# Six half-array matmuls in place of four whole-array ones in the rotary part of the attention scores of a hybrid encoder layer

## The reference, cut to what matters

```
q_b = concat([q_b[..., :128], rope(q_b[..., 128:], positions)], -1)
k_b = concat([k_b[..., :128], rope(k_b[..., 128:], positions)], -1)
s = einsum('bhqd,bhkd->bhqk', qblk, k_t) / sqrt(192)
p = softmax(s, -1)
o = einsum('bhqk,bhkd->bhqd', p, v_t)
```

## Time and profile before

| | |
|---|---|
| median of 3 runs | 1947.18 us (1946.17 to 1947.29) |
| the profiled execution: span from first to last instruction | 1945.4 us |
| PE busy | 1877.6 us, 97% |
| PE weight loads | 1593.0 us, 82% |
| DVE busy | 1391.9 us, 72% |
| ACT busy | 1049.2 us, 54% |
| granted TensorE clock, mean | 0.987 |

### The profile page before, as it was taken

How to read it: one execution, slowest core, us unless ns; L and a number is a source line. 1 busy time by engine, 2 the same in 40 slices (tenths; PEclk the granted TensorE clock), 3 DMA queues, 4 the chain that set the end, 5 groups by cost and what they waited for, 6 DMA issues and landing times.

```text
span 1945.4 us, 26995 instructions
## 1 busy us (share of the span) xinstructions
PE 1877.6 (97%) x9388; PEld 1593.0 (82%) x9388; DVE 1391.9 (72%) x1955; ACT 1049.2 (54%) x1726; POOL 135.6 (7%) x147
## 2 busy tenths in 40 slices
PE   7999999999999999999999999994799999999998
PEld 7988888888878888888888888884688888888886
DVE  4578777778855656657766348646799898998986
ACT  6476566555552434344434223321577777877775
POOL 1121101011000000000000000000000101001010
PEclk9999999999999999999999999997899999999999
DMA  6110000000321202022344463534899999999993
GB/s 208 44 43 6 24 23 18 23 23 20 125 61 33 66 22 68 20 76 87 123 165 147 150 197 109 192 130 194 320 377 400 391 401 399 390 400 389 400 391 77
DMA packets 147480, 327.55 MB, mean 168 GB/s; under 512 B 18080, under 2 KB 72736, under 8 KB 147232
## 3 DMA queue, kind: packets, MB, share of 16 engines
q1 hardware_dynamic: 142640, 309.59, 42.9%
q0 software_dynamic: 4752, 16.78, 3.4%
HBM read 287.92 MB, written 38.40 MB: 168 GB/s over the span
## 4 chain that ended last, share of the span: by engine, by line
PE 91%; DVE 5%; ACT 2%; issue 1%; DMA 1%; POOL 1%; SPq 0%; DVEq 0%; ACTq 0%; POOLq 0%
PE ps L1078 24%; PE ps L1080 24%; PE ps L1079 24%; PE ps L1067 7%; PE ps L1163 4%; PE ps L1371 1%; PE ps L1202 1%; PE ps L1201 1%; PE ps L1383 1%; PE ps L1355 1%; PE ps L1525 1%; PE ps L1381 1%; DVE top_i L2476 1%; DVE top_v L2475 1%; DVE affT L2478 1%
## 5 line engine op out<-in xcount | busy, mean ns | idle before, releaser
L1649 DVE TENSOR_TENSOR w_lo<-w_raw,w_hi 128x1024 fp32r<-128x1024 f32 x384 | 442.7, 1220 | 54.8 <-ACT w_hi L3052 54.7
L3052 ACT ACTIVATE w_hi<-w_raw 128x1024 fp32r<-128x1024 f32 x384 | 370.8, 1053 | 12.1 <-DMA w_raw<-in_w_gate_e 11.8
L1078 PE MATMUL ps<-w_hi,xeT_hi 128*128 128x512 f32 x512 | 201.2, 393 | 1.8 <-DVE xeT_lo L1649 1.0
L1080 PE MATMUL ps<-w_hi,xeT_lo 128*128 128x512 f32 x512 | 199.7, 390 | 0.0
L1079 PE MATMUL ps<-w_lo,xeT_hi 128*128 128x512 f32 x512 | 199.2, 389 | 0.0
L1649 DVE TENSOR_TENSOR d_lo<-d_raw,d_hi 128x1024 fp32r<-128x1024 f32 (+1 forms) x66 | 67.2, 1028 | 124.9 <-ACT d_hi L2714 120.3
L1078 PE MATMUL ps<-hT_parts,d_hi 128*128 128x512 f32 x368 | 145.2, 395 | 0.0
L1080 PE MATMUL ps<-hT_parts,d_lo 128*128 128x512 f32 x368 | 144.1, 392 | 0.0
L1079 PE MATMUL ps<-hT_parts,d_hi 128*128 128x512 f32 x368 | 144.0, 391 | 0.0
L985 POOL TENSOR_TENSOR stat<-stat,minus_half 128x4 f32<-128x4 f32 (+3 forms) x56 | 54.2, 969 | 1180.1 <-DVE stat L1646 1180.0
L1884 DVE TENSOR_REDUCE row_max<-ps 128x1 f32<-128x1024 f32 x64 | 78.3, 1224 | 79.1 <-PE ps L1202 79.0
(11 more groups left out here) (436 smaller groups left out, 4332.4 us busy)
## 6 DMA issues: line engine op xcount, KB each, us to landing
w_raw<-in_w_gate_e SPq DMA_DIRECT2D x128, 512.0 KB, 7.0
w_raw<-in_w_up_e SPq DMA_DIRECT2D x128, 512.0 KB, 7.1
w_raw<-in_w_down_e SPq DMA_DIRECT2D x128, 512.0 KB, 5.8
d_raw<-in_w_in SPq DMA_DIRECT2D x80, 256.0 KB, 3.2
gates_T<-stage SPq DMA_DIRECT2D x16, 512.0 KB, 2.6
sg<-gates_T SPq DMA_DIRECT2D x16, 512.0 KB, 3.7
stage<-mla_out_T SPq DMA_DIRECT2D x12, 512.0 KB, 5.1
xs<-in_x SPq DMA_DIRECT2D x8, 512.0 KB, 12.6
```

What stands on the lines that cost most here:

```text
L1078: pe.matmul(out_ap, a_hi, b_hi, start=start, stop=False)
L1080: return pe.matmul(out_ap, a_lo, b_hi, start=False, stop=stop)
L1649: return dve.tensor_tensor(dst, whole, high.bitcast(F32), ALU.subtract)
L3052: nc.scalar.activation(w_hi[:, n % RING, :], w_raw[:, n % RAW, :], ACT.Copy).then_inc(hi_ok, 1)
```

## The change

In each score tile the plain part comes first for both banks. Then the rotary part follows as six matmuls over 64 rows each: high·high, high·low, low·high, and within each of these the first bank and then the second. The first bank's operands lie on partitions 0 to 63 (rows 0 to 63 of the array), the second bank's on partitions 64 to 127.

The operands are laid out for that. `qr_T` becomes `qr_hi` and `qr_lo`, each with all 64 elements on both halves of the partitions. `kr_T` becomes `kr_hi`; this and `kr_lo` hold keys 0 to 511 on partitions 0 to 63 and keys 512 to 1023 on partitions 64 to 127, so each is half as wide. ACT's and DVE's operations of a seam follow: the rotary part of q has its low part made on 128 partitions, where it was 64, and the rotary part of k has its two parts made on 64 partitions, where it was 128. Low·low is no longer added.

```diff
-                        qr_T = sb_in(head_mem, "qr_T", [P, S], F32R)
+                        qr_hi = sb_in(head_mem, "qr_hi", [P, S], F32R)
+                        qr_lo = sb_in(head_mem, "qr_lo", [P, S], F32R)
...
-                        kr_T = (d_lo[:, 0, :], sb_in(head_mem, "kr_T", [P, S], F32R)[:])
-                        kr_lo = (d_lo[:, 1, :], sb_in(head_mem, "kr_lo", [P, S], F32R)[:])
+                        kr_hi = (d_lo[:, 0, 0:HALF], sb_in(head_mem, "kr_hi", [P, HALF], F32R)[:])
+                        kr_lo = (d_lo[:, 1, 0:HALF], sb_in(head_mem, "kr_lo", [P, HALF], F32R)[:])
...
+                q = slice(n * P, (n + 1) * P)
                 for j in range(2):
                     cols = slice(j * HALF, (j + 1) * HALF)
-                    bank = ps[:, 2 * (n % 2) + j, :]
-                    q = slice(n * P, (n + 1) * P)
-                    three(bank, qT_hi[:, q], qT_lo[:, q], kT_hi[i % 2][:, cols], kT_lo[i % 2][:, cols], True, False)
-                    pe.matmul(bank, qr_T[:, q], kr_T[i % 2][:, cols], start=False, stop=False)
-                    mm = pe.matmul(bank, qr_T[:, q], kr_lo[i % 2][:, cols], start=False, stop=True)
+                    three(ps[:, 2 * (n % 2) + j, :], qT_hi[:, q], qT_lo[:, q], kT_hi[i % 2][:, cols],
+                          kT_lo[i % 2][:, cols], True, False)
+
+                for m, (a, b) in enumerate(((qr_hi, kr_hi), (qr_hi, kr_lo), (qr_lo, kr_hi))):
+                    for j in range(2):
+                        rows = slice(j * ROPE, (j + 1) * ROPE)
+                        mm = pe.matmul(ps[:, 2 * (n % 2) + j, :], a[rows, q], b[i % 2][rows], start=False, stop=m == 2)
                 mm.then_inc(s_mm, 1)
...
-                    ins = low_part(qr_T[ROPE:P, cols], ps[ROPE:P, bank, :], qr_T[ROPE:P, cols])
+                    ins = low_part(qr_lo[:, cols], ps[:, bank, :], qr_hi[:, cols])
                 else:
-                    ins = low_part(kr_lo[h % 2][:, cols], ps[:, bank, :], kr_T[h % 2][:, cols])
+                    rows = slice(half * ROPE, (half + 1) * ROPE)
+                    ins = low_part(kr_lo[h % 2][rows], ps[rows, bank, :], kr_hi[h % 2][rows])
...
-                    ins = nc.scalar.activation((qr_T, kr_T[h % 2])[what // 2][:, cols], src, ACT.Copy)
+                    rows = slice(half * ROPE, (half + 1) * ROPE)
+                    ins = nc.scalar.activation(kr_hi[h % 2][rows], src[rows], ACT.Copy)
```

More of the change, by code:

```diff
@@ L2687, in seam_high @@
                                                scale=(qhn_c, khn_c)[what // 2][:, 0:1])
-                else:
-                    ins = nc.scalar.activation((qr_T, kr_T[h % 2])[what // 2][:, cols], src, ACT.Copy)
+                elif what == 1:
+                    ins = nc.scalar.activation(qr_hi[:, cols], src, ACT.Copy)
+                else:
+                    rows = slice(half * ROPE, (half + 1) * ROPE)
+                    ins = nc.scalar.activation(kr_hi[h % 2][rows], src[rows], ACT.Copy)
                 ins.then_inc(seam_hi, 1)
```

## The result

| | before | changed |
|---|---|---|
| median | 1947.18 us (5 runs, 1946.17 to 1947.95) | 1954.56 us (5 runs, 1954.26 to 1954.67) |
| ratio | | 1.0039, 95% interval 1.0028 to 1.0049 |
| span of the profiled execution | 1945.4 us | 1952.3 us |
| PE busy | 1877.6 us | 1884.5 us |

The change costs 7.4 us. Its direction was forecast; the forecast was +23 us, so the size was three times too large. The range, 1933 to 1979 us, held it only because it also took in the rival without a drain: the likeliest case's own range, 1958 to 1979, did not.

What follows compares the result with a forecast made beforehand. PE was taken to bound the kernel. Per tile, −0.92 removed, +0.80 for six matmuls and 2 × (0.13 + 0.11) for shape changes give +0.36 us, times 64 +23 us: 1947.2 + 23 = 1970 us, range 1933 to 1979.

Steps and rivals of the forecast that it cites:

- the rival without a drain: Score tiles: pairs run at once, shape changes cost nothing; 8 to 15 us faster, 1932 to 1939 us; chance 0.31.
- the likeliest case: Score tiles: matmuls run in pairs and changing rows drains the array; forecast 1970 us, range 1958 to 1979; chance 0.50.
- PE sets the pace: Heads' stretch: PE busy 392.0 of 395 us, so its gains or losses count whole; 0.1 us per tile is 6.4 us.
- The matmuls run in pairs: Score tile's six 64-row matmuls: two on different rows and banks run at once; one after another they would take 1.38 us.
- With the loads one by one: Six 64-row matmuls: a pair's second waits 0.11 us for its weights, so the six take 0.80 us per tile.
- The drain at each change of rows: Score tile, 128 to 64 rows and back: array empties, d = 0.13 us each time, bounds 0.09 and 0.17.
- The load itself is no longer hidden: First 64-row matmul and first transpose after the six: an exposed weight load of 0.11 us at each change.
- perfect pairs: Six 64-row matmuls: both of every pair fully at once, 0.69 us per tile, 0.11 less than the 0.80 taken.
- The sum: Per score tile: −0.92 + 0.80 + 2 × (0.13 + 0.11) = +0.36 us; times 64, +23 us.
- DVE and ACT cost nothing: Seams in the heads: reshaped operations keep 512 columns and their durations, 680 to 694 and 598 ns; no cost.
- no pairs (2, 3): Score tiles: six matmuls run singly; without drain +29 us, 1977, chance 0.06; with drain +60 us, 2007, chance 0.09.
- no effect (4): Score tiles: shape changes cost by chance near 0.12 us, or a new wait takes the gain; no change; chance 0.04.

Runs made afterwards that it cites:

- e1: The kernel before with each tile's rotary part as four matmuls over rows 0 to 63 alone, low·high left out: 1967.56 us, ratio 1.0108.
- e3: The changed kernel without the third 64-row pair, so low·high of the rotary part is left out: 1941.72 us, ratio 0.9971.
- e2: The changed kernel with its twelve matmuls reordered so each pair stands between plain ones, six shape changes per tile in place of two: 2003.28 us, ratio 1.0285.
- e8: The changed kernel with the rotary pairs ahead of the six plain matmuls of a tile: 1957.13 us, ratio 1.0050.
- e5: The changed kernel with its six 64-row matmuls listed bank by bank, three on each half of the rows: 1954.66 us, ratio 1.0036.

## Why the prediction was right in its direction and wrong in its size

- **PE sets the pace, and what it loses goes through whole.** Right, but for the first head. The heads' stretch grew by 6.7 us, the span by 6.9, the median by 7.4.
- **The matmuls run in pairs.** Right, though no row of before showed it, as the prediction says; e1 against e3 does. The page on TensorE (the Trainium skill, TensorE: Matmul & The Clock Gate, Part 3) says it too, and the trace agrees: two starts in one row at 294.18, 3 ns apart.
- **"With the loads one by one": 0.80 us for the six. Wrong: 0.70.** This term failed first. The 0.11 us pace of the loader was measured on loads into the same rows. Loads into different halves of the rows run together (x2, 0.19 us), so the bound called perfect pairs, 0.69, was the true one. 0.10 us per tile, 6.4 us.
- **The drain at each change of rows.** Right in kind: both places where it was to show, show it, 64 and 61 times, and e2 multiplies it. The Trainium skill (TensorEngine Tiling (Array Packing), Key Properties) names it, and the 0.36 us of idle loader agree. Its size was too large: 0.09 and 0.10 us in place of 0.13. That is the lower of the two bounds, in which the whole 0.17 us of the earlier trace rows scales with the clock; I had gone to the middle. (Whether it is the clock that makes the difference is not shown: the shapes differ too.) 0.07 us per tile, 4.5 us.
- **"The load itself is no longer hidden": 0.11 us at each change. Half right.** 0.11 at the entry. At the exit it is 0.06, because a transpose follows there; the earlier trace rows priced it on a float32r matmul. e8, which ends a stay in front of a float32r matmul, costs 0.04 to 0.05 us more per tile. 0.05 us per tile, 3.2 us.
- **The sum.** 0.36 − 0.10 − 0.07 − 0.05 = +0.14 us per tile, 9 us. The stretch grew by 2.3 us less than that: 0.8 us of it is the first head, where PE waits for others and the steps lengthen by 0.34 us in place of 1.1, and the rest is the 0.12 us that the other heads' steps show on average in place of 0.14. So the size is explained by terms that all erred to the same side: where the working gave two ends, I chose the middle or the upper one. Even all lower ends together, perfect pairs and d = 0.09, give +0.17 per tile and the 1958 us at which the likeliest case's own range began; below that lie the load after the exit, which had been given no range, and the first head.
- **DVE and ACT cost nothing.** Right. The low part of q on 128 partitions takes 692 ns (694 on 64 in the earlier trace rows) and that of k on 64 partitions 689 (680 on 128), ACT's high part of k 592 (598):

```profile
L1653 DVE TENSOR_TENSOR qr_lo<-ps,qr_hi x16: 683/692/694, 125.0 to 500.8; 128x512 fp32r<-128x512 f32 x16
L1653 DVE TENSOR_TENSOR kr_lo<-ps,kr_hi x8: 673/689/696, 148.7 to 481.6; 64x512 fp32r<-64x512 f32 x8
...
L2697 ACT ACTIVATE kr_hi<-ps x8: 592/592/594, 147.8 to 480.4; 64x512 fp32r<-64x512 f32 x8
```

- **The rivals.** No drain (1) is refuted by the two stalls and e2; no pairs (2, 3) by e1 against e3; no effect (4) by the interval, 1.0028 to 1.0049. What stays open: why the drain is as long as it is, and whether it differs between other shapes; only 128 to 64 and back was tried, and 32 to 128 once in the trace. That the array is emptied in it is a reading too: what the trace shows is a load that starts 0.32 us after the last matmul's start, which is before the recorded end of that matmul (0.40 us).

## What to carry to other kernels

Two matmuls on disjoint halves of the array's rows cost as much as one, but entering and leaving that shape costs 0.35 to 0.40 us, more than one and a half matmuls of 512 columns. Count the stays: by these numbers a stay has to save two whole matmuls to pay, and here it saved one (four became three pairs). Merging the stays of two tiles was to earn half of the price back, 11 us; it earned 5.0, and 8.3 with one seam moved. Then look at what the shortened step starved, step by step against the trace of before, and not by the sum of a wait: here ScalarE's squares were waited for 25 times and it mattered in step 5 of the heads, and a shift of 1.4 to 2.1 us in all odd steps to help them cost 15 us elsewhere.

## What the runs showed of the hardware that I had not expected

- Weight loads into different halves of the rows run at the same time (both in 0.19 us), while loads into the same rows are 0.11 us apart.
- Matmuls on different halves of the rows do not wait for each other's turn in the list: in e5 the fourth of six starts 0.01 us after the first, at no loss (1954.66 against 1954.56 us). The Trainium skill (TensorE: Matmul & The Clock Gate, Part 3) has matmuls starting in strict order; e5's trace shows that order only within a half.
- The drain at a change of rows: 0.09 to 0.10 us between 128 and 64 rows at the 2.4 GHz level, whatever stood before it (e8), and 0.17 us from 32 to 128 rows at the 1.2 GHz one (once, in the trace of before), plus a weight load that is not made ahead (0.11 us before a float32r matmul, 0.06 before a transpose).
